# Three stage seams of a two-layer hybrid block: an FFN weight tile split earlier, a head's Q, K and V loaded earlier, side products re-spread

## The reference

```python
for i in range(2):
    mod = silu(c) @ ada_w[i] + ada_b[i]              # six vectors; the same for c_ctx
    P = modulate(LN(x), mod[0], mod[1]) @ w_in[i]    # q, k, v, f, cs, co, gate
    cs, co = token_shift(P.cs), token_shift(P.co)    # p + mu0*(prev-p) + mu1*(next-p)
    decay = f(w0 + tanh(cs.w) @ w2);  a = sigmoid(a0 + cs.a @ a2)
    kk = l2norm_per_head(cs.k * k_k);  o_c = two_directional_recurrence(...)
    o_a = differential_attention(rope(q), rope(k), v, context prefix)
    o_f = fft2(P.f)
    y = sum_of_three(sigmoid(gate) * (o @ w_p)) @ w_o
    x = LN(alpha * x + mod[2] * y)
    u, g = modulate(LN(x), mod[3], mod[4]) @ ffn_up
    x = LN(alpha * x + mod[5] * ((gelu(dwconv3(g)) * u) @ ffn_down))
```

## Time and profile before

| what | value |
|---|---|
| median of 3 runs | 3583.35 us (3582.41 to 3583.75) |
| the profiled execution | 3584.85 us, its span 3583.10 us |
| PE busy | 3339.7 us, 93% of the span |
| DVE, ACT, POOL busy | 1559.7, 1294.5, 1104.0 us (44%, 36%, 31%) |

### The profile page before, as it was taken

How to read it: one execution, slowest core, us unless ns; L and a number is a source line. 1 busy time by engine, 2 the same in 40 slices (tenths; PEclk the granted TensorE clock), 3 DMA queues, 4 the chain that set the end, 5 groups by cost and what they waited for, 6 DMA issues and landing times. The chain is left out here.

```text
span 3583.1 us, 82852 instructions
## 1 busy us (share of the span) xinstructions
PE 3339.7 (93%) x36717; PEld 2683.2 (75%) x36717; DVE 1559.7 (44%) x2509; ACT 1294.5 (36%) x2253; POOL 1104.0 (31%) x697
## 2 busy tenths in 40 slices
PE   6999999999888999999999899999999898889998
PEld 4668888888765777787878676787777666678887
DVE  4244344443277646412112734444544386461324
ACT  3332233333266424421212143334343365343322
POOL 2111132232111533332333132214333213445553
PEclk8999999999999999999999999999999999999999
DMA  7663423442221543233332145334442323523332
GB/s 256 226 208 105 117 85 109 127 126 82 90 77 33 166 137 121 71 118 120 116 121 95 46 143 183 104 106 129 126 122 89 105 82 118 166 90 101 100 94 88
DMA packets 444862, 420.81 MB, mean 117 GB/s; under 512 B 15652, under 2 KB 372042, under 8 KB 437594
## 3 DMA queue, kind: packets, MB, share of 16 engines
q1 hardware_dynamic: 442922, 406.73, 36.3%
q10 hardware_dynamic: 1584, 8.78, 0.6%
HBM read 326.72 MB, written 88.74 MB: 116 GB/s over the span
## 5 line engine op out<-in xcount | busy, mean ns | idle before, releaser
L898 PE MATMUL ps<-I-321_h_hi,I-324_w_hi 128*128 128x512 f32 (+1 forms) x1376 | 510.9, 371 | 9.3 <-PEq L126 9.2
L898 PE MATMUL ps<-I-322_h_lo,I-324_w_hi 128*128 128x512 f32 (+1 forms) x1376 | 486.1, 353 | 1.7 <-issue 1.7
L898 PE MATMUL ps<-I-321_h_hi,I-325_w_lo 128*128 128x512 f32 (+1 forms) x1376 | 484.7, 352 | 0.0
L375 PE MATMUL ps<-I-321_h_hi,I-324_w_hi 128*128 128x512 f32 (+1 forms) x1448 | 432.3, 359 | 11.7 <-POOL I-325_w_lo L2558 9.4
L2558 POOL TENSOR_TENSOR I-325_w_lo<-I-323_w_raw,I-324_w_hi 128x1024 fp32r<-128x1024 f32 x118 | 283.9, 2406 | 504.3 <-ACT I-324_w_hi L2521 504.3
L375 PE MATMUL ps<-I-321_h_hi,I-325_w_lo 128*128 128x512 f32 (+1 forms) x1448 | 425.2, 354 | 0.0
L375 PE MATMUL ps<-I-322_h_lo,I-324_w_hi 128*128 128x512 f32 (+1 forms) x1448 | 423.0, 352 | 0.0
L862 POOL TENSOR_TENSOR I-325_w_lo<-I-323_w_raw,I-324_w_hi 128x1024 fp32r<-128x1024 f32 x68 | 168.0, 2471 | 599.9 <-ACT I-324_w_hi L1142 599.8
L2521 ACT ACTIVATE I-324_w_hi<-I-323_w_raw 128x1024 fp32r<-128x1024 f32 x120 | 127.2, 1060 | 547.1 <-PE ps L375 342.7
L375 PEld LDWEIGHTS ps<-I-321_h_hi,I-324_w_hi 128*128 128x128 f32 x1448 | 236.3, 189 | 92.8 <-issue 42.8
L898 PEld LDWEIGHTS ps<-I-321_h_hi,I-324_w_hi 128*128 128x128 f32 x1376 | 263.7, 192 | 51.4 <-issue 10.5
(11 more groups left out here) (899 smaller groups left out, 6998.5 us busy)
## 6 DMA issues: line engine op xcount, KB each, us to landing
I-323_w_raw<-in_w_in SPq DMA_DIRECT2D x134, 512.0 KB, 5.5
I-323_w_raw<-in_ffn_up SPq DMA_DIRECT2D x88, 512.0 KB, 3.9
I-19222_ada_w<-in_ada_w SPq DMA_DIRECT2D x24, 1024.0 KB, 5.9
I-323_w_raw<-in_ffn_down SPq DMA_DIRECT2D x44, 512.0 KB, 3.3
proj_d<-I-2005_result SPq DMA_DIRECT2D x52, 384.0 KB, 2.9
I-513_ada_w<-in_ada_w SPq DMA_DIRECT2D x16, 1024.0 KB, 5.5
I-330_gate<-proj_d SPq DMA_DIRECT2D x24, 384.0 KB, 3.3
proj_d<-I-25070_result SPq DMA_DIRECT2D x36, 256.0 KB, 2.2
```

The costliest lines, as they stand in the source:

```text
L375: m = pe.matmul(dst[:, at:at + n], w[wi][:, k, :], a[ai][:, k, at:at + n], start=k == 0 and i == 0, stop=k == kt - 1 and i == 2)
L898: m = pe.matmul(bank(6 + i % 2, n_c), w[:, k, :], hv[:, k, c0:c0 + n_c], start=k == 0 and v == 0, stop=k == KT - 1 and v == 2)
```

## The change

First layer of `rwkv_inputs`: two adaLN steps stand behind tiles 0 and 1 and one behind tiles 2 to 13, so the first run of eight ends behind tile 5 and the second behind tile 13; the copies stand behind tiles 5 and 13, the first flip behind tile 7. In both layers the spreads stand at p = 22, 25, 27, 28, the second eight low-rank products at 18, 19, 20, 21, 23, 24, 26, 29, and SP's stores of kk ahead of the last tile's store. The first head's five loads are issued in the recurrence, after the store of the fourth last filler, into buffers laid over inputs of the recurrence (`placed`). The third FFN weight tile is split at the end of `close`, by ACT and DVE, once the first tile's opening has ended (`f_used`), and the opening follows four tiles behind in place of two (`LAG`).

```diff
-            LORA = {p: i for i, p in enumerate((*range(6, 14), *range(19, 27)))}
+            LORA = {p: i for i, p in enumerate((*range(6, 14), 18, 19, 20, 21, 23, 24, 26, 29))}
-            SPREAD = {p: t for t, p in enumerate((27, 28, 29, 30))}
+            SPREAD = {p: t for t, p in enumerate((22, 25, 27, 28))}
+            beside_lora = {t: sum(q < p for q in LORA) for p, t in SPREAD.items()}
+            beside_kk = {i: sum(q < p for q in SPREAD) for p, i in LORA.items()}
...
+                ada_at = {n: (2 * n, 2 * n + 1) if n < 2 else (n + 2,) for n in range(len(ada) - 2)}
...
-                        if ada:
-                            ada_load(sp, sem, ring, n, ada[n])
+                        for e in ada_at.get(n, ()):
+                            ada_load(sp, sem, ring, e, ada[e])
...
-                        if n >= 13:
-                            store_lora(n - 9)
+                        if n >= 12:
+                            store_lora(n - 8)
...
                     store(N - 3)
-                    store_lora(6)
+                    store_kk(0)
+                    store_kk(1)
                     store(N - 2)
+                    store_kk(2)
+                    store_kk(3)
                     store_lora(7)
                     store(N - 1)
-                    for t in range(CTILES):
-                        sp.wait_ge(sem("kk_done"), t + 1)
-                        sp.dma_start(raw_d[:, R_KK + t, :], kk[:, t, :]).then_inc(sem("raw_out"), 16)
...
+                            if beside_kk[i]:
+                                pe.wait_ge(sem("kk_done"), beside_kk[i])
...
-                            pe.wait_ge(sem("lora"), 16)
+                            pe.wait_ge(sem("lora"), beside_lora[t])
...
-                        if ada and n == 8:
-                            ada_copy(act, sem, 0, 6)
+                        if ada and n in (5, 13):
+                            ada_copy(act, sem, n // 8, 6)
...
+                        for p in (2 * n - 1, 2 * n):
+                            if p in SPREAD:
+                                normed(SPREAD[p])
                         dve.wait_ge(sem("own"), n + 1)
...
+                    def first_head():
+                        sp.wait_ge(sem("tmm"), 8 * N_G)
+                        sp.wait_ge(sem("pmm"), 2 * sum(n_pr))
+                        sp.wait_ge(sem("rk"), y_before(N_G))
+                        sp.wait_ge(sem("rot_out"), 16 * len(turned))
+                        for p in range(2):
+                            sp.wait_ge(sem(f"stored{p}"), 16 * len(range(p, len(slots) - 5, 2)))
+                        q_tok = SEQ if last else TOK
+                        for dst, src in ((kr0[:, :], rot_d[HA]), (qr0[:, :], rot_d[0]), (kp0[:, :], proj_d[J_K, :, SEQ:TOK]),
+                                         (qp0[:, 0:q_tok], proj_d[J_Q, :, 0:q_tok]), (vp0[:, :], proj_d[J_V])):
+                            sp.dma_start(dst, src).then_inc(first_in, 16)
...
+                        if s == len(slots) - 4:
+                            first_head()
                     put_y(N_G - 1)
...
                         if n == 0:
-                            pe.wait_ge(sem("q_first"), 32)
...
+                            pe.wait_ge(first, 16 * 5)
...
-                    sp.wait_ge(sem("f_in2"), 16)
...
-                    for j in range(KT + 2):
+                    LAG = 4
+                    for j in range(KT + LAG):
...
                         for k in range(KT):
                             pe.wait_ge(sem("n_lol"), k + 1)
-                            opening(s, 1, k, OF_HI + OF_LO)
+                            m = opening(s, 1, k, OF_HI + OF_LO)
+                        m.then_inc(sem("f_used"), 1)
...
+                    act.wait_ge(sem("f_in2"), 16)
+                    act.wait_ge(sem("f_used"), 1)
+                    act.activation(rings[1][:, 0], rings[0][:, 2], ACT.Copy).then_inc(sem("f_hi"), 1)
...
+                    dve.wait_ge(sem("f_hi"), 3)
+                    dve.tensor_tensor(rings[2][:, 0], rings[0][:, 2], rings[1][:, 0].bitcast(F32), ALU.subtract)
...
-            DONE = 2
-            lo_count = lambda g: g + 1 - DONE - sum(e < g for e in by_dve)
+            DONE, SPLIT = 2, 3
+            lo_count = lambda g: g + 1 - SPLIT - sum(e < g for e in by_dve)
...
-                        if g + 2 < N:
+                        if SPLIT <= g + 2 < N:
                             split(g + 2)
```

More of the change, by code:

```diff
@@ L599, in _ @@
                         beside(2 * n + 1)
[L600 to L603, removed]
+                        for e in ada_at.get(n, ()):
+                            ada_step(pe, sem, ring, e, 6)
+                        if ada and n == 7:
+                            ada_flip(pe, sem, 0, 7)
                     if ada:
-                        ada_step(pe, sem, ring, N, 6)
                         ada_flip(pe, sem, 1, 7)
-                    beside(2 * N)
                 @block.scalar
@@ L690, in rwkv_inputs, with rwkv_scan @@
             return N
-        def rwkv_scan(l, s2, h, rings, o_w, last, late):
+        def rwkv_scan(l, s2, h, rings, o_w, last, late, first_in):
             G = [P, GCOL]
@@ L1357, in _, with attention @@
                                 dve.tensor_tensor(y, y, half(2 * d).rearrange("p i (t c) -> p t i c", t=CTILES), ALU.add).then_inc(sem("Ysum"), 1)
-        def attention(l, oq, sm, ss, rings, last, late):
+            return qr0, kr0, qp0, kp0, vp0
+        def attention(l, oq, sm, ss, rings, last, late, first, head0):
             nq = LT if last else NT
@@ L1373, in attention @@
             v_part = {(j, part + 1): part for j in range(HA - 1) for part in range(2)}
-            with ExitStack() as sc, stage(nc, (late,)) as (block, sem):
+            with ExitStack() as sc, stage(nc, (late, first)) as (block, sem):
                 qp = sb(sc, "q_plain", [P, 2, TOK])
@@ L1391, in _ @@
                     src = A["w_pa"][l].rearrange("(k p) n -> p k n", p=P)
-                    for j in range(HA):
+                    for j in range(1, HA):
                         if j >= 2:
@@ L1443, in scores @@
                             j, u = units[n]
+                            qrj, krj = of_head(j)[0:2]
                             if u < LT:
-                                pe.matmul(score(n, c, SEQ), qr[half(c), j % 2, u * P:(u + 1) * P], kr[half(c), j % 2, :],
+                                pe.matmul(score(n, c, SEQ), qrj[half(c), u * P:(u + 1) * P], krj[half(c), :],
                                           start=True, stop=True)
@@ L1448, in scores @@
                             j, u = units[n]
-                            pe.matmul(score(n, c, CTX_LEN, SEQ if u < LT else 0), qp[half(c), j % 2, u * P:(u + 1) * P],
-                                      kp[half(c), j % 2, :], start=True, stop=True).then_inc(sem(f"s{c}_mm"), 1)
+                            qpj, kpj = of_head(j)[2:4]
+                            pe.matmul(score(n, c, CTX_LEN, SEQ if u < LT else 0), qpj[half(c), u * P:(u + 1) * P],
+                                      kpj[half(c), :], start=True, stop=True).then_inc(sem(f"s{c}_mm"), 1)
                     def turn(n, n_v):
@@ L2661, in program @@
             with ExitStack() as sc:
-                late = nc.alloc_semaphore(f"late_stores{l}")
+                late, first = nc.alloc_semaphore(f"late_stores{l}"), nc.alloc_semaphore(f"first_head{l}")
                 with ExitStack() as s2:
@@ L2665, in program @@
                     with ExitStack() as s3:
-                        rwkv_scan(l, s3, h, rings, n_w, last, late)
+                        head0 = rwkv_scan(l, s3, h, rings, n_w, last, late, first)
                 with ExitStack() as s2:
@@ L2671, in program @@
                     ss = sb(s2, "ss", [P, n_heads])
-                    attention(l, oq, sm, ss, rings, last, late)
+                    attention(l, oq, sm, ss, rings, last, late, first, head0)
                     merge_pa(l, oq, sm, ss, oc, y, gt, rings, last)
```

76 lines of the change are left out of this document (35 added, 41 removed).

## The result

The changed kernel takes 3548.76 us (median of 5 runs, 3543.43 to 3552.38) against 3582.41 us of the kernel before beside it (5 runs, 3579.76 to 3583.75). The ratio is 0.9905, 95% interval 0.9894 to 0.9915: 33.7 us less, where 31.7 us had been forecast. The profiled execution is the fastest of the five: 3543.43 us, span 3541.60. Against the profiled execution of before it lies 41.4 us lower (3584.85 - 3543.43), so that about 8 us of what the two traces show belong to these two executions and not to the kernels. The experiments come back to that.

A forecast was written before the change was run, and what follows sets the result against it. PE was taken as the bound, busy 3339.7 of 3583.1 us, with its waits and slow-clock stretches to be won. The terms sum to 31.7 us, which from the median 3583.35 gives 3551.7 us, range 3546 to 3566.

The forecast's parts named there:

- A, wait and slow stretch: First layer's inputs: PE's 4.8 us wait for the adaLN row's copy and 1.7 us of slow clock go, 6.5 us.
- A and B, first layer's inputs whole: First layer's inputs: 6.5 us from the moved adaLN steps plus 1.7 us from a shorter tail before the recurrence.
- B, second layer: End of the second layer's inputs: with spreads moved ahead, the tail before the recurrence takes 9.0 against 11.83 us, gaining 2.8.
- C: Start of attention: with the first head's operands already loaded, PE begins 4.15 us sooner in each layer, 8.3 together.
- D, first layer: FFN start, first layer: 3.5 us of wait for tile 2's split go and the kept clock gives 2.5, 6.0 us.
- D, second layer: FFN start, second layer: tile 3 reached 5.7 us sooner, limited by its own low part, ready at 3221.95.
- lag: Closing stage: the opening's longer lag removes part of 3.0 us of waits for rounded columns, taken as 0.7 us.
- I expect this clock to stay: First 13.1 us of attention: the granted clock of 0.52 was expected unchanged, so it was given no value.
- Rival 1: FFN starts: the clock falls all the same, leaving 27.0 us of gain, 3556.4 us; chance 0.20.
- Rival 2: Inputs: new waits, at tile 2's load or among spreads and low-rank products, leave 3 of 11 us; 3559.7 us, chance 0.12.
- rival 3: Attention: the first head's transfers did not hold it, so 8.3 us are lost; 3560.0 us, chance 0.12.
- Rival 4: Recurrence: SP waits inside the first head's loads and PE's fillers stop, making the kernel slower, 3591.4 us at 55 us; chance 0.04.

The follow-up runs named there:

- A: Kernel before with only the moved adaLN steps of the first layer's inputs, without the spreads, low-rank products and kk stores; 3572.95 us (1 run).
- C: Kernel before with only the first head's five loads issued in the recurrence; 3568.66 us, ratio 0.9969.
- D: Kernel before with only the third FFN tile split in the closing stage and the opening four tiles behind; 3567.76 us, ratio 0.9961.
- half: Changed kernel with the third FFN tile's low part made by DVE at the start of ffn, not in the closing stage; 3548.49 us (1 run).
- preload: Changed kernel with FFN's tiles 3 and 4 loaded at the end of the closing stage; 3547.32 us, ratio to the kernel before 0.9907.
- again: Changed kernel unedited, run and profiled a second time; 3548.67 us, ratio to the kernel before 0.9912.
- late_head: Changed kernel with the first head's five loads issued behind the last filler's store, ahead of the store of y; 3562.11 us (1 run).
- AB: Kernel before with only the changes in the inputs: adaLN steps, spreads, low-rank products and kk stores; 3570.84 us, ratio 0.9965.
- lag2: Changed kernel with the opening two tiles behind, as before, in place of four; 3544.44 us (1 run).

## Why the prediction was right

The place of each gain was as forecast: the waits that were to go are gone, FFN starts at the full clock, and each part alone shows its gain. The median came out 2.9 us below the predicted time, within the range. That it came so close is in part luck: most terms came out smaller than forecast, and a gain that no term has made up for it. Term by term, from the distances above:

| term | forecast | measured |
|---|---|---|
| A, wait and slow stretch | 6.5 | 6.8 (A alone) |
| A and B, first layer's inputs whole | 8.2 | 7.4 to 7.6 |
| B, second layer | 2.8 | 1.6 |
| C | 8.3 | 8.4, and 0.8 to 1.6 inside the first attention |
| D, first layer | 6.0 | 5.6 |
| D, second layer | 5.7 | 4.5 to 5.0 |
| lag | 0.7 | 0.7 |
| sum, without the first row | 31.7 | 28.4 to 28.7, with the attention's 29.6 to 30.1 |

The sum of the distances (A and B of the first layer are in it once, taken whole) stays 3.6 to 5.3 us short of the 33.7 us between the medians, and below the interval of the ratio, 30.5 to 38.0 us. About 1 us of that can be read off: the lower level that the first layer's recurrence starts in lasts 6.0 us of it before and 3.2 after (3.0 to 4.8 in the profiles that have part B, 4.7 to 6.1 in the others). More of it may lie in the recurrences. In the eight profiles with part B they took 718.4 and 612.2 us in the mean, in the four without it 721.8 and 613.4, 4.6 us more together, and the low level behind the stop 42 us in came in one of the eight and in all of the four. But single profiles of one kernel lie up to 5 us apart there, so that twelve of them don't show whether this is the change or chance.

What was mis-sized:

- B's step "from there the store, its landing and the barrier, as they lay behind the last kk before" took 3.5 us; it is 4.2. The last store is no longer alone: the store of the last sigmoids, 768 KB, goes out 1.5 us ahead of it. Taking that store away gave 0.54 us back in both layers, which shows the larger part; the other 0.15 us stay open. In the second layer tile 14's products also end 2.6 us later where 2.3 had been put. And the 11.8 us of the tail before, from which the term was taken, hold a low clock (the last spread took 2.89 us there, where the others took 1.55, as in the earlier trace rows); C and D have the same, but A's profile, with that layer unchanged, has 2.03 us for that spread and a tail of 10.9 us, against which B's gain there would be 0.8 us.
- D in the second layer: "tile 3's own low part was ready at 3221.95" was a bound from ACT's list, 7.5 us behind the stage's start. The bound is now the load: issued at the start of the stage, it lands 5.4 us later, and the low part is ready 8.9 us behind it. Loading the tile in the closing stage took the wait away, which shows the cause. Why the load takes longer than the 4.0 us (at most) in which it was there before was not separated. Three loads now go out together, where the third waited for a split before, and in half, where it waits again, the first lands after 4.05 us; but in preload the one load of the stage's start takes 5.3 us by itself.
- D in the first layer: the 3.5 us of wait went as forecast (4.71 to 1.20); the clock gave 2.1 to 2.3 us in place of 2.5.
- C's "I expect this clock to stay": in the first layer the first 13.1 us run at 0.74 (0.61 in `again`) in place of 0.52, and the attention is 1.6 (0.8) us shorter, as its length goes with that clock in all profiles. What keeps the clock up stays open: late_head has 0.70, with a stop of 9 us ahead of it, so the shorter stop is not the cause, or not the only one; and in the second layer the kernel before has 0.76.

Rival 1 did not come: in all fourteen FFN starts of the seven profiles with a stop of 1.2 us the clock stayed at 1.00, and in all eight of the four with a stop of 4.7 us it was low for 2.9 to 5.5 of the first 5.5 us. half shows how near it was: at 2.5 us it is one of two. The Trainium skill (TensorE: Matmul & The Clock Gate, Part 1) says that the number of slow matmuls varies from run to run, because the gate's observation isn't tied to the program; the two layers of half, with the same stop, and the two profiles of the changed kernel, with 0.74 and 0.61 at the start of the first attention, agree with it. Rival 2 is refuted in its first form by A, and in its second by AB, where PE has no wait at the low-rank products or the spreads; rival 3 is refuted by C. Rival 4 did not come either: SP was through with the five loads at 910.51 and next wanted at 921.69, 11 us of room; what its list costs without such room late_head shows.

## What to carry to other kernels

At a seam of stages, look for the one thing that the next stage's first product waits for and do it in the last stage under work that is there anyway; the gain is the distance from the barrier to that product, and in late_head it was lost when the issue lay where its queue was busy and the wait took in a load that the first product does not need. Behind each such gain ask for what is next in line (the second load, the store that is no longer alone), since here it took 0.5 to 1.4 us back. Where runs differ by more than a part is worth, compare distances inside one stage over several profiles, and don't credit the change with a difference in a stretch whose program is the same unless several profiles of both kernels agree on it.

## What the runs showed that I had not expected

- One unchanged stretch of program differs by 5 us between executions: the recurrence of the first layer took 716.2 us (lag2) to 721.5 us (preload) in kernels that have the same program there, by the length of a handful of stops of 2 to 5 us and the level of the clock behind them.
- DVE's 128 x 16 scaling of the adaLN row (L216) took 1.77 us at the end of the changed kernel's inputs, where POOL's subtraction of a 128 x 1024 tile was under way when it began, and 0.17 us before, where it was not. In all eight profiles with this order it ended 0.03 us behind that subtraction; DVE's addition just ahead of it (L212) took 0.18 us beside the same subtraction.
